# Forget bias as one f32r matmul, gates broadcast by DMA, two more ada buffers and a negated row maximum in a two-layer encoder trunk

## The chip, the cores and the metric

The kernel runs on one core of a Trainium2 chip. The metric is the device time of one execution in microseconds, lower is better. Inputs lie in HBM when it starts, and the output is written back to HBM.

## The reference

The input x is 256 x 2048 in fp32. Two layers, each a token mixer and a dense SwiGLU FFN, with six modulation vectors a layer made from the conditioning vector c:

```python
c_act = silu(c)
for i in range(2):
    mod = c_act @ ada_w[i] + ada_b[i]
    sh_a, sc_a, g_a, sh_f, sc_f, g_f = split(mod, 6)
    h = x * (1 + sc_a) + sh_a
    y = mla(h) if i == 0 else fox(h)
    x = layer_norm(ALPHA * x + (1 + g_a) * y)
    h = x * (1 + sc_f) + sh_f
    y = (silu(h @ w1) * (h @ w3)) @ w2
    x = layer_norm(ALPHA * x + (1 + g_f) * y)
```

MLA has 16 heads with a rotary part and a mask by chunks of 64. FoX (forgetting attention) has 16 heads of 128, a causal mask, and adds `cum[q] - cum[k]` to the scores, where cum is the running sum of log sigmoid of a forget logit for each head. In a softmax over k the term cum[q] falls out, so only a row of -cum[k] has to be added.

## The kernel before

Everything is computed in fp32 precision. A weight matrix comes in **units** of 256 rows by 512 columns (MLA's query weights 384), 512 KB each. SP loads a unit into one of four `raw` slots, ACT rounds it to f32r (`whi`, L503), DVE takes the rest (`wlo`, L852), and PE multiplies: activations as weights (`hT_hi`, `hT_lo`), the unit as moving data, 8 matmuls with `whi` (L1405) and 4 with `wlo` (L1411). ACT and DVE split up to four units ahead (`ahead`), each wait being on a semaphore.

The order of work on each engine is written out by hand. It goes: 16 chunks of MLA's down projection, MLA projections (32 units), MLA attention, output projection `w_o` (32 units), `norm_turn` (layer norm, turning x by PE transposes and affine), FFN (264 units), then the same with FoX. Attention runs in 19 **ticks** (`attention`), one head per tick and stage: tick i turns q and k of head i, scores head i-1, turns p of head i-2 and multiplies by v for head i-3, with units between (`gap`, by `tick_gaps`): two per tick, or six in FoX's first twelve.

Scores of a FoX head (L1579 to L1587) are four fp32 matmuls: q by k for both query tiles, and after each the bias, with 16 rows on the contraction side: a column of `ident` that picks the head, over `cumT` (16 x 256). An MLA head has the rotary part in that place (L1582). DVE adds the mask and takes the row maximum (L1189), waits for itself and multiplies by -scale (`nmax`, L1194); ACT takes exp from it (L709).

The **ada sums** are the 192 dot products of 128 rows of `ada_w` (1 MB each) with silu(c): POOL issues the loads in order (L455), each into the buffer that `ADA_SLOT` names, when the sum before in that buffer is done; DVE makes the sum (L876). The first 32 come before everything. From number 54 there are three buffers, among them `gate`, and from 64 two. The sums up to number 79 must be done before the first `norm_turn`; they stand between the other work on DVE: two a tick up to tick 16 and none in the last two, six in `w_o` and two behind it.

The **gate** (1 + g, as a column `mod`) has to stand along a row on all partitions. PE makes it by 16 fp32 matmuls of 128 columns in four parts, a broadcast column times `ident` (`gate_turn`, L1391), and ACT copies each part from PSUM (`gate_copy`, L650). This is done four times: in ticks 16 to 18 of both attentions, and in the first block of the first down product of both FFNs. DVE then uses it in `residual` (L960, L967) and `weigh` (L988). In layer 0 ACT multiplies x by ALPHA in two instructions at ticks 1 and 3 (L702); in the other sub-layers this is part of `scale_xa`.

## Time and profile before

| what | value |
|---|---|
| runs (three) | 2312.52 us median, 2311.64 to 2314.25 |
| the profiled execution: its own time, its span | 2319.15 us, 2317.4 us |
| PE busy | 2207.6 us (95%) |
| DVE, ACT busy | 1572.6 us (68%), 1009.2 us (44%) |
| HBM read | 597.49 MB, 259 GB/s over the span |
| chain of work that ended last | PE 82%, DVE 8%, DMA 7%, ACT 2%, issue 1% |

A share of busy time is a mean over stages. The stages here are: 0 to 134 us ada sums and down projection, to 303 us the MLA projections and attention up to tick 16, to 375 us its end and `w_o`, to 406 us the first norm turn, to 1128 us the first FFN, to 1510 us the FoX projections and attention, to 1556 us `w_o`, and then the second FFN to the end. Starts on PE's timeline are the better measure of a matmul's cost, since consecutive ones overlap: the row's own duration includes its way through the array.

### The profile page before, as it was taken

The page shows a single profiled execution, that of the slowest core. Times are in us where ns is not written, and L with a number is a line of the kernel's source. Part 1 is how long each engine was busy: PE and PEld are TensorE (multiplying, and loading weights), DVE is VectorE, ACT ScalarE, POOL GpSimd, SP SyncE. Part 2 cuts the span into 40 slices and gives each one's busy share as a digit, 9 for nine tenths or more (in the row PEclk, how much of TensorE's full clock was granted, in tenths as well). Part 3 has the DMA queues.
Part 4 walks back from the last instruction along what each step waited for, and adds up shares of the span by engine and source line. Part 5 has one row for each costly group of instructions (what it writes and reads, how often), then busy time and mean ns, then how long its engine had stood idle before and what let it go on. Part 6 is the DMA issues. An engine that isn't in the chain of part 4 may idle for free.

```text
span 2317.4 us, 25362 instructions
## 1 busy us (share of the span) xinstructions
PE 2207.6 (95%) x9962; PEld 1797.4 (78%) x9962; DVE 1572.6 (68%) x1799; ACT 1009.2 (44%) x1331; POOL 104.5 (5%) x207
## 2 busy tenths in 40 slices
PE   4789997999999999999999999999999999999997
PEld 2377785888888888888788888777888888888885
DVE  5779988877758777768875555568775454554556
ACT  1056644444444344444544444545444343444433
POOL 2110100000000000000000000000000000000000
PEclk9989998999999999999999999999999999999998
DMA  9988986788869888888567666656876466666563
GB/s 390 418 332 316 350 324 234 270 297 295 303 223 338 323 323 293 298 322 328 208 230 245 215 213 213 210 191 232 299 288 195 157 201 198 192 190 190 187 228 121
DMA packets 137192, 601.27 MB, mean 259 GB/s; under 512 B 15601, under 2 KB 15857, under 8 KB 111089
## 3 DMA queue, kind: packets, MB, share of 16 engines
q1 hardware_dynamic: 109424, 398.31, 49.0%
q0 software_dynamic: 27648, 201.34, 23.7%
q8 instruction: 79, 1.29, 0.2%
q14 instruction: 41, 0.33, 0.0%
HBM read 597.49 MB, written 2.10 MB: 259 GB/s over the span
## 4 chain that ended last, share of the span: by engine, by line
PE 82%; DVE 8%; DMA 7%; ACT 2%; issue 1%; POOL 0%; SPq 0%; ACTq 0%; DVEq 0%; POOLq 0%
PE ps L1405 50%; PE ps L1411 25%; DMA ada_head<-in_ada_w 4%; DVE wlo L852 2%; DVE ada_w L876 2%; PE ps L1421 2%; DMA ada_w<-in_ada_w 1%; DMA raw<-in_mla_w_o 1%; PE ps L1380 1%; PE ps L1579 1%; PE ps L1587 1%; DVE ada_wide L876 1%; PE ps L1391 1%; ACT whi L503 1%; DVE ada_head L876 1%
## 5 line engine op out<-in xcount | busy, mean ns | idle before, releaser
L852 DVE TENSOR_TENSOR wlo<-raw,whi 128x1024 fp32r<-128x1024 f32 (+2 forms) x721 | 873.4, 1217 | 641.1 <-ACT whi L503 640.4
L503 ACT ACTIVATE whi<-raw 128x1024 fp32r<-128x1024 f32 (+2 forms) x721 | 758.7, 1054 | 1096.6 <-PE ps L1411 982.5
L1405 PE MATMUL ps<-whi,hT_hi 128*128 128x512 f32 x1880 | 586.4, 393 | 0.0
L1405 PE MATMUL ps<-whi,hT_lo 128*128 128x512 f32 x1880 | 579.9, 390 | 0.0
L1411 PE MATMUL ps<-wlo,hT_hi 128*128 128x512 f32 x1880 | 502.9, 389 | 0.0
L1405 PEld LDWEIGHTS ps<-whi,hT_lo 128*128 128x128 f32 x1880 | 352.9, 188 | 74.2
L1411 PEld LDWEIGHTS ps<-wlo,hT_hi 128*128 128x128 f32 x1880 | 352.9, 188 | 74.0
L1405 PEld LDWEIGHTS ps<-whi,hT_hi 128*128 128x128 f32 x1880 | 347.9, 188 | 72.6 <-issue 3.5
L876 DVE CUSTOM_DVE_ANT_0 ada_w<-ada_w,c_bc,cols 128x2048 f32<-128x2048 f32 x153 | 358.9, 2346 | 27.8 <-DMA ada_w<-in_ada_w 27.8
L1405 PE MATMUL ps<-whi,uT_hi 128*128 128x512 f32 x672 | 208.1, 391 | 3.3 <-ACT whi L503 3.3
L1405 PE MATMUL ps<-whi,uT_lo 128*128 128x512 f32 x672 | 207.0, 389 | 0.0
L1411 PE MATMUL ps<-wlo,uT_hi 128*128 128x512 f32 x672 | 179.6, 389 | 0.0
L1405 PEld LDWEIGHTS ps<-whi,uT_hi 128*128 128x128 f32 x672 | 125.3, 188 | 29.1 <-ACT whi L503 3.6
L455 POOL DMA_DIRECT2D ada_w<-in_ada_w x153 | 80.9, 529 | 1465.2 <-DVE mod L876 1453.2
L1405 PEld LDWEIGHTS ps<-whi,uT_lo 128*128 128x128 f32 x672 | 126.1, 188 | 26.3
L1411 PEld LDWEIGHTS ps<-wlo,uT_hi 128*128 128x128 f32 x672 | 126.1, 188 | 26.3
L1701 PE MATMUL ps<-down_w,h 128*128 128x512 f32 x128 | 71.9, 689 | 22.3 <-ACT h L772 19.5
L1701 PEld LDWEIGHTS ps<-down_w,h 128*128 128x128 f32 x128 | 24.8, 216 | 43.9 <-ACT h L772 22.1
L876 DVE CUSTOM_DVE_ANT_0 ada_head<-ada_head,c_bc,cols 128x2048 f32<-128x2048 f32 x17 | 40.0, 2351 | 17.0 <-DMA ada_head<-in_ada_w 16.9
L772 ACT ACTIVATE h<-ps,mod 128x256 f32<-128x256 f32 x16 | 8.9, 564 | 84.4 <-DVE mod L876 72.3
L1421 PE MATMUL ps<-whi,hT_hi 128*128 128x512 f32 x72 | 32.5, 452 | 5.9 <-issue 3.9
L668 ACT ACTIVATE p_sb<-p_sb,pinv 128x128 f32<-128x128 f32 x64 | 25.7, 451 | 26.4 <-DVE pinv L1203 26.3
(228 smaller groups left out, 1528.0 us busy)
## 6 DMA issues: line engine op xcount, KB each, us to landing
raw<-in_ffn_w SPq DMA_DIRECT2D x528, 512.0 KB, 4.3
ada_w<-in_ada_w POOLq DMA_DIRECT2D x153, 1024.0 KB, 6.1
raw<-in_fox_w_in SPq DMA_DIRECT2D x96, 512.0 KB, 3.6
ada_head<-in_ada_w POOLq DMA_DIRECT2D x17, 1024.0 KB, 21.8
raw<-in_mla_w_o SPq DMA_DIRECT2D x32, 512.0 KB, 7.4
raw<-in_fox_w_o SPq DMA_DIRECT2D x32, 512.0 KB, 3.6
gate<-in_ada_w POOLq DMA_DIRECT2D x14, 1024.0 KB, 9.2
down_w<-in_mla_w_down SPq DMA_DIRECT2D x16, 544.0 KB, 8.0
```

The source lines that it names most:

```text
L455: pool.dma_start(ada_buffer(n), A["ada_w"][l, q, c]).then_inc(ada_in[ADA_SLOT[n]], 16)
L503: nc.scalar.activation(whi[:, s, 0:n], raw[:, s, 0:n], ACT.Copy).then_inc(hi_ready, 1)
L668: ins = nc.scalar.activation(p_sb[:, g % 2, a:b], p_sb[:, g % 2, a:b], ACT.Copy, scale=pinv[:, g % 2, t:t + 1])
L852: nc.vector.tensor_tensor(wlo[:, s, 0:n], raw[:, s, 0:n], whi[:, s, 0:n].bitcast(F32), ALU.subtract).then_inc(lo_ready, 1)
L876: nc.vector.tensor_tensor_reduce(w, w, c_bc[:, :], 1.0, adab_col[:, q, c:c + 1], ALU.mult, ALU.add, mod[:, q, c:c + 1]).then_inc(ada_done, 1)
L1380: ins = nc.tensor.transpose(ps[:, 4 + pl.turn % 2, o:o + P], tile(t, c0 + c), ident[:, :])
L1391: ins = nc.tensor.matmul(ps[:, bank, c * P:(c + 1) * P], column.to_broadcast([P, P]), ident[:, :], start=True, stop=True)
L1405: nc.tensor.matmul(ps[:, 2 * pair + t, 0:width], a[:, t * P:(t + 1) * P], w_hi, start=(first and c == 0 and a is hi), stop=False)
L1411: ins = nc.tensor.matmul(ps[:, 2 * pair + t, 0:width], hi[:, t * P:(t + 1) * P], w_lo, start=False, stop=(end and c == UC - 1))
L1421: ins = nc.tensor.matmul(ps[:, 2 * pair + t, :], a[:, t * P:(t + 1) * P], w, start=(first and c == 0 and a is hi), stop=(end and c == UC - 1))
L1579: nc.tensor.matmul(o, qkT[:, m % 2, q], qkT[:, m % 2, S:S + n], start=True, stop=False)
L1701: nc.tensor.matmul(ps[:, 2 * which + t, :], a, w[:, which * LORA:(which + 1) * LORA], start=(c == 0), stop=(c == KC - 1))
```

## The change

- **FoX bias.** `cumT` becomes `cum`, f32r, 128 rows of which 48 are used: -cum in rows 0 to 15 rounded to f32r, what the rounding left in rows 32 to 47, the three blocks of key columns (128 and 256) side by side. The cumulative sum is made for both copies from `logf_twin`. `pick` has a one in both rows of a head. One f32r matmul of 384 columns comes first in the head's scores and opens the accumulation; the two q by k matmuls add to it.
- **Gates.** `gate_turn`, `gate_copy` and `gate_parts` are gone. ACT issues a DMA (`gate_out`) that writes the column `mod` (128 x 16, fp32) as a row of 2048 into HBM, element by element, at tick 12 of both attentions and in the next to last block of each FFN's first pass, and later a DMA (`gate_in`) that reads this row onto all 128 partitions (1 MB), at tick 16 and in the first block of the down product.
- **Ada sums.** The gate buffer serves up to number 61, and 62 to 79 use four buffers: two new ones (`ada_low`, over the latents' space, free when all 32 MLA projections are done) and the two old ones. One sum stands earlier on DVE (before the latents' variance), the last two ticks have one each, `w_o` has five, and none stands behind it.
- **Maximum.** The mask pass has the factor -scale and takes the minimum, so that it gives `nmax` itself, and exp has scale -1. DVE's `nmax` instruction and its wait for itself are gone.
- **ALPHA** of layer 0 is applied in the residual's addition (`add_to`), and the two ACT instructions are gone.

```diff
@@ ada_slots
         elif n < ADA_GATE_UNTIL:
             slots.append((2, 0, 1)[(n - ADA_WIDE_UNTIL) % 3])
+        elif n < ADA_LOW_UNTIL:
+            slots.append((9, 10, 0, 1)[(n - ADA_GATE_UNTIL) % 4])
         else:
             slots.append(n % 2)
@@ constants, buffers, loads of POOL
-ADA_GATE_UNTIL = 64
+ADA_GATE_UNTIL = 62
+ADA_LOW_UNTIL = 80
+    ada_low = place_at("ada_low", [P, 2, D], F32, b0)
-    cumT = new("cumT", [H, S])
+    cum = new("cum", [P, 3 * P], F32R)
+    pick = new("pick", [P, H], F32R)
+    logf_twin = new("logf_twin", [P, T, TWIN + H])
+                if ADA_SLOT[n] >= 9:
+                    pool.wait_ge(units_used, PROJ[0])
@@ ACT
-            def gate_copy(part, bank):
...
+            def gate_out(layer, q):
+
+                act.wait_ge(ada_done, ada_end(layer, q))
+                act.dma_start(rows[pl.gate].rearrange("(c p) -> p c", p=P), mod[:, layer * MODS + q, :],
+                              allow_slow_non_contiguous=True).then_inc(gate_row, 16)
                 pl.gate += 1
+            def gate_in():
+
+                act.wait_ge(gate_row, 16 * pl.gate)
+                act.dma_start(gate[:, :], rows[pl.gate - 1].partition_broadcast(P)).then_inc(gate_copied, 16)
@@ ACT, attention
-                    if rotary and i in (1, 3):
...
-                        nc.scalar.activation(xa[:, t, :], xa[:, t, :], ACT.Copy, scale=ALPHA
-                                             ).then_inc(xa_scaled, 1)
-                                                       bias=nmax[:, m % 2, t:t + 1], scale=scale,
+                                                       bias=nmax[:, m % 2, t:t + 1], scale=-1.0,
-                    for part, bank in gate_parts(i):
...
+                    if i == H - 4:
+                        gate_out(layer, G_A)
+                    if i == H:
+                        act.wait_ge(ada_done, ada_last(2))
+                        gate_in()
@@ ACT, ffn
+                        if (n, i) == (0, nb - 2):
+                            gate_out(l, G_F)
                     if n == 0:
-                        for part in range(4):
-                            gate_copy(part, 6 + part % 2)
+                        gate_in()
@@ DVE
+            def add_to(x, y, raw):
+
+                if raw:
+                    return nc.vector.scalar_tensor_tensor(out=x, in0=x, scalar=ALPHA, in1=y,
+                                                          op0=ALU.mult, op1=ALU.add)
+                return nc.vector.tensor_tensor(x, x, y, ALU.add)
-                dve.wait_ge(gate_copied, pl.gate)
+                dve.wait_ge(gate_copied, 16 * pl.gate)
-                                p_sb[:, m % 2, a:b], ps[:, 5, a:b], mask[:, a:b], 1.0,
-                                -3.0e38, ALU.add, ALU.max, smax[:, m % 2, t:t + 1])
+                                p_sb[:, m % 2, a:b], ps[:, 5, a:b], mask[:, a:b], -scale,
+                                3.0e38, ALU.add, ALU.min, nmax[:, m % 2, t:t + 1])
-                        dve.wait_ge(masked, m + 1)
-                        nc.vector.tensor_scalar(nmax[:, m % 2, :], smax[:, m % 2, :], -scale, None,
-                                                ALU.mult).then_inc(max_ready, 1)
-                    if layer == 0 and i < TICKS - 2:
+                    if layer == 0:
                         ada()
+            ada()
             dve.wait_ge(ssq_ready, 1)
@@ PE
+                        if not rotary:
+                            nc.tensor.matmul(ps[:, 5, 0:3 * P], pick[:, i - 1:i].to_broadcast([P, P]),
+                                             cum[:, :], start=True, stop=False)
...
-                                head = ident[0:H, i - 1:i]
-                                ins = nc.tensor.matmul(o, head.to_broadcast([H, P]), cumT[:, 0:n],
-                                                       start=False, stop=True)
-                    for part, bank in gate_parts(i):
...
-                        gate_turn(layer, G_A, part, bank)
```

On PE, in the scores of one FoX head (`qkT` q and k turned, `cumT` and `cum` the bias rows). Before:

```order
L1411 MATMUL ps<-wlo,hT_hi 128x512 x4
L1579 MATMUL ps<-qkT 128x128
L1587 MATMUL ps<-cumT,ident 128x128
L1579 MATMUL ps<-qkT 128x256
L1587 MATMUL ps<-cumT,ident 128x256
L1405 MATMUL ps<-whi,hT_hi 128x512 x2
```

And now:

```order
L1423 MATMUL ps<-wlo,hT_hi 128x512 x4
L1588 MATMUL ps<-cum,pick 128x384
L1593 MATMUL ps<-qkT 128x128
L1593 MATMUL ps<-qkT 128x256
L1417 MATMUL ps<-whi,hT_hi 128x512 x2
```

The two bias matmuls are one, ahead of the q by k matmuls. On DVE, from the third residual of MLA's `w_o` to the first norm turn (the ISA rows on `mod` are the ada sums). Before:

```order
L971 BN_STATS stats<-xa 128x6 x2
L852 TENSOR_TENSOR wlo<-raw,whi 128x1024
L876 ISA ada_w,mod<-ada_w,c_bc,cols 128x2048
L876 ISA mod 128x1
L852 TENSOR_TENSOR wlo<-raw,whi 128x1024 x2
L876 ISA ada_w,mod<-ada_w,c_bc,cols 128x2048
L876 ISA mod 128x1
L852 TENSOR_TENSOR wlo<-raw,whi 128x1024
L876 ISA ada_w,mod<-ada_w,c_bc,cols 128x2048
L876 ISA mod 128x1
L876 ISA ada_w,mod<-ada_w,c_bc,cols 128x2048
L876 ISA mod 128x1
```

And now:

```order
L985 BN_STATS stats<-xa 128x6 x2
L859 TENSOR_TENSOR wlo<-raw,whi 128x1024
L883 ISA ada_low,mod<-ada_low,c_bc,cols 128x2048
L883 ISA mod 128x1
L859 TENSOR_TENSOR wlo<-raw,whi 128x1024 x3
L992 TENSOR_TENSOR gcol<-cols,mod 128x16
L994 TENSOR_TENSOR gcol<-cols,mod 128x16
L996 TENSOR_TENSOR gcol<-gcol,mod 128x16
```

Of four sums in this place one is left, and the columns of the norm turn follow the last split directly.

## Rows read from the trace of the kernel before

**Rows 1.** The page, part 1: busy time, share, instructions
```profile
PE 2207.6 (95%) x9962; PEld 1797.4 (78%) x9962; DVE 1572.6 (68%) x1799; ACT 1009.2 (44%) x1331; POOL 104.5 (5%) x207
```

**Rows 2.** Chain that ended last, in first FFN: start us, us, what
```profile
463.80 1.81 PE ps L1405 x8
466.51 1.81 PE ps L1405 x8
```

**Rows 3.** Busy us (instructions) of PE, PEld, DVE, ACT, POOL; clock; DMA share; GB/s
```profile
138.00:303.00 165.00, 152.97 (x806) 133.26 (x805) 155.70 (x258) 105.58 (x219) 17.94 (x34) 0.97 0.87 327
303.00:375.00 72.00, 65.53 (x300) 53.17 (x299) 57.99 (x66) 26.78 (x35) 5.28 (x10) 1.00 0.87 324
1167.00:1510.00 343.00, 343.00 (x1580) 275.60 (x1579) 195.41 (x277) 167.48 (x275) 11.09 (x21) 1.00 0.65 225
```

**Rows 4.** Waits of PE: total us, times, longest us
```profile
PE ps L1463 <- issue: 10.0, 3, 9.4
PE ps L1566 <- DVE hT_lo L1174: 9.7, 5, 3.8
PE ps L1421 <- DVE wlo L852: 8.2, 7, 1.7
```

**Rows 5.** PE timeline, one FoX head's scores: start us, us, instruction
```profile
1272.95 0.38 PE L1579 MATMUL ps<-qkT 128*128 128x128 f32 x2
1273.27 0.48 PE L1587 MATMUL ps<-cumT,ident 16*128 16x128 f32 x2
...
1275.50 0.63 PE L1405 MATMUL ps<-whi,hT_lo 128*128 128x512 f32 x2
```

**Rows 6.** PE timeline, one MLA head's scores
```profile
289.15 0.38 PE L1579 MATMUL ps<-qkT 128*128 128x128 f32 x2
289.37 0.39 PE L1582 MATMUL ps<-kpT,qpT 128*128 128x128 f32 x2
...
290.02 0.59 PE L1582 MATMUL ps<-kpT,qpT 128*128 128x256 f32 x2
...
290.92 0.63 PE L1405 MATMUL ps<-whi,hT_lo 128*128 128x512 f32 x2
```

**Rows 7.** PE timeline, f32r matmuls of 384 columns, two each
```profile
159.74 0.51 PE L1405 MATMUL ps<-whi,qlT_lo 128*128 128x384 f32 x2
160.09 0.51 PE L1405 MATMUL ps<-whi,qlT_hi 128*128 128x384 f32 x2
```

**Rows 8.** PE timeline, gate matmuls of first FFN
```profile
669.48 1.05 PE L1391 MATMUL ps<-ident,mod 128*128 128x128 f32 x8
...
683.10 0.73 PE L1405 MATMUL ps<-whi,uT_hi 128*128 128x512 f32 x2 [1.63 <-ACT whi L503]
```

**Rows 9.** PE timeline, gate matmuls of FoX attention
```profile
1502.92 1.95 PE L1391 MATMUL ps<-ident,mod 128*128 128x128 f32 x16
1504.62 0.70 PE L1405 MATMUL ps<-whi,hT_hi 128*128 128x512 f32 x2
```

**Rows 10.** The costliest groups of DVE, by line
```profile
L1194 DVE TENSOR_SCALAR nmax<-smax 128x2 f32<-128x2 f32 x32 | 5.4, 170 | 1.1
```

**Rows 11.** DVE timeline before the first norm turn
```profile
370.67 2.35 DVE L876 CUSTOM_DVE_ANT_0 ada_w<-ada_w,c_bc,cols 128x2048 f32<-128x2048 f32 x1 [2.22 <-DMA ada_w<-in_ada_w]
...
379.54 0.69 DVE L988 TENSOR_TENSOR sums<-ps,gate 128x512 f32<-128x512 f32 x1
```

**Rows 12.** PE timeline, start of the first and the third norm turn
```profile
384.12 1.94 PE L1463 MATMUL ps<-ident,xa 128*128 128x128 f32 x8 [9.39 <-issue]
...
1556.88 1.06 PE L1463 MATMUL ps<-ident,xa 128*128 128x128 f32 x8 [0.30 <-issue]
```

**Rows 13.** DMA: queue (packets, MB, share), issue (count, KB, us to landing)
```profile
q1 hardware_dynamic: 109424, 398.31, 49.0%
...
c_bc<-in_c SPq DMA_DIRECT2D x1, 1024.0 KB, 4.7
```

**Rows 14.** SP timeline, one small issue
```profile
1.73 0.42 SPq L368 DMA_DIRECT2D pos_i<-in_pos  x1
```

More of the change, by code:

```diff
@@ L62 @@
 FOX_CUM = 2 * PAIRS + 3
+TWIN = 32
 ADA_HEAD = 2 * KC
@@ L151, in two_pi_parts, with trunk @@
     return parts + [float(np.float32(left))]
-def trunk(nc, A, out):
+def trunk(nc, A, rows, out):
     x_d = A["x"][0].rearrange("(t p) d -> p t d", p=P)
@@ L287, in trunk @@
         down_in = [sem(f"down_in{i}") for i in range(DOWN_SLOTS)]
-        ada_in = [sem(f"ada_in{i}") for i in range(9)]
+        ada_in = [sem(f"ada_in{i}") for i in range(11)]
         raw_in = [sem(f"raw_in{i}") for i in range(RING)]
@@ L799, in _ @@
                     pl.turn += 1
-            attention(0, MLA_SCALE)
+            attention(0)
             w_o()
@@ L817, in _ @@
                     pl.turn += 1
-            attention(1, FOX_SCALE)
+            attention(1)
             w_o()
@@ L1207, in w_o @@
             def w_o(layer):
-                pl.gate += 4
-                if layer == 0:
-                    dve.wait_ge(xa_scaled, T)
+                pl.gate += 1
                 for b in range(2):
                     pl.pe += 1
-                    residual(b, True)
+                    residual(b, True, layer == 0)
                     ahead()
@@ L1218, in w_o @@
                         ada()
-                residual(2, True)
+                residual(2, True, layer == 0)
                 for k in range(PAIRS - SPLIT):
                     units(1)
-                    if layer == 0 and k in (0, 2):
+                    if layer == 0 and k == 0:
                         ada()
@@ L1353, in _ @@
                     dve.wait_ge(turned, pl.turn + 1)
-                    nc.vector.tensor_scalar(cumT[:, :], ps[0:H, 4 + pl.turn % 2, 0:S], -1 / FOX_SCALE,
-                                            None, ALU.mult).then_inc(turned_out, 1)
+                    own()
+                    for a, b in ((0, P), (P, 3 * P)):
+                        mark(nc.vector.tensor_scalar(cum[0:TWIN + H, a:b],
+                                                     ps[0:TWIN + H, 4 + pl.turn % 2, 0:b - a],
+                                                     -1 / FOX_SCALE, None, ALU.mult))
+                    own()
+                    for a, b in ((0, P), (P, 3 * P)):
+                        low = cum[TWIN:TWIN + H, a:b]
+                        ins = nc.vector.scalar_tensor_tensor(
+                            out=low, in0=ps[TWIN:TWIN + H, 4 + pl.turn % 2, 0:b - a],
+                            scalar=-1 / FOX_SCALE, in1=low.bitcast(F32), op0=ALU.mult, op1=ALU.subtract)
+                    ins.then_inc(turned_out, 1)
                     pl.turn += 1
@@ L1383, in turn @@
                 pl.turn += 1
-            def gate_turn(layer, q, part, bank):
-                pe.wait_ge(ada_done, ada_end(layer, q))
-                for c in range(4):
-                    n = 4 * part + c
-                    column = mod[:, layer * MODS + q, n:n + 1]
-                    ins = nc.tensor.matmul(ps[:, bank, c * P:(c + 1) * P],
-                                           column.to_broadcast([P, P]), ident[:, :],
-                                           start=True, stop=True)
-                ins.then_inc(gate_turned, 1)
-                pl.gate += 1
             def unit(pair, width, parts, first, end):
@@ L1825 @@
     out = nc.dram_tensor("out", (1, S, D), F32, kind="ExternalOutput").ap()
-    trunk(nc, A, out)
+    rows = nc.dram_tensor("gate_rows", (2 * LAYERS, D), F32).ap()
+    trunk(nc, A, rows, out)
     r = run_bass_kernel_spmd(nc, [{f"in_{n}": a for n, a in arrays.items()}], core_ids=[0])
```

76 lines of the change are left out of this document (29 added, 47 removed).

## The prediction

> **What bounds the kernel now.** Read the page's busy line first: PE is busy for 2207.6 us, 95% of the span [rows 1]. So nearly everywhere an instruction taken from PE shortens the run by its own pitch (start to start), and the time of DVE, ACT or the DMA queues counts only where PE idles. The chain of waits shows the steady state of an FFN: a unit every 2.71 to 2.72 us and nothing between [rows 2]. Then the windows [rows 3]. In FoX's projections and attention, to its last ticks, PE is busy for 343.00 of 343.00 us and DVE for 195.41: PE alone is the bound. In MLA's projections and attention (138 to 303 us) DVE is busy for 155.70 of 165.00 us, PE for 152.97, and DMA is 0.87 used: three resources nearly full, and none waits long for any one cause. From 303 to 375 us (last ticks and `w_o`) PE has 65.53 of 72.00 us. Last, PE's waits [rows 4]: the largest that the change touches is one of 9.4 us ahead of L1463, the first norm turn.
>
> Durations below come from the profiled execution, whose own time is 2319.15 us. The median of the runs is 2312.52, so 6.6 us less; I subtract the sum from both. About 0.2% (5 us) is what a measurement of this kernel can tell from no change.
>
> **1. FoX bias on PE.** One head's scores with the first two f32r matmuls behind them take from 1272.95 to 1275.50, so 2.55 us [rows 5]. An MLA head has four matmuls of the same columns, all with 128 rows, and takes 290.92 - 289.15 = 1.77 us for the same stretch [rows 6]. The difference, 0.78 us, is what the two bias matmuls with 16 rows cost beyond their columns. Without the second and third of the MLA matmuls there would be 0.22 us for q by k of 128 columns (289.15 to 289.37) and 0.90 us for 256 columns and the two f32r ones behind (290.02 to 290.92). The new matmul is f32r over 384 columns: two of those take 0.35 us, so 0.17 each [rows 7]. New total 0.17 + 0.22 + 0.90 = 1.29 us, 1.26 less than now. Sixteen heads: **20.2 us**. PE has no idle in this stage, so all of it counts. If the 16 rows had no price of their own, the saving would be 1.77 - 1.29 = 0.48 us a head, 7.7 us in all: the lower end. A rule stands against my reading here. The Trainium skill says in "TensorE: Matmul & The Clock Gate", section "LDWEIGHTS (loading the stationary operand)", that a 32x128 weight load takes the same time as one of 128x128. By that page the 16 rows cost nothing of their own; the 0.78 us above speaks against it.
>
> The DVE work that comes with it (a second copy of the log forget, two set-ups, three more small instructions on the cumulative sum) I cost at nothing. The cumulative sum is taken ten units after the forget logits, ten times 2.72 us, and DVE is idle for 43% of this stage [rows 3]. Without that cover it would be some 2 us, once.
>
> **2. Gates in the FFNs.** From the first gate matmul to the unit behind the last part it is 683.10 - 669.48 = 13.62 us, in which three units are done, 8.16 us [rows 2, 8]. So 5.46 us are the gate's: 16 matmuls and 1.63 us in which PE waits for ACT's split, since ACT stood at its gate copies. Two FFNs: **10.9 us**. The split then comes in time, as ACT no longer waits for PE there.
>
> **3. Gate in FoX attention.** Eight of the matmuls (16 records, as an fp32 matmul leaves two) take 1504.62 - 1502.92 = 1.70 us [rows 9]; sixteen take **3.4 us**, on PE's bound.
>
> **4. Layer 0 up to the first norm turn.** Here more than PE counts.
> - `nmax` took 0.17 us and its wait some 0.04 [rows 10]: 16 times 0.21 = 3.4 us of DVE, in a stage where DVE is 94% busy. I take 2.5. In the FoX stage it hides under PE and counts nothing.
> - The last ticks and `w_o`: 3.4 us of gate matmuls go, and some of the waits for `wlo` (8.2 us in all of the run [rows 4]), as the last four units have one ada sum beside them in place of two. Against it, two more sums (2.35 us each) stand in the last two ticks. PE has only 6.5 us of idle there [rows 3]. I take 4.0, with ends 0 and 9.
> - The norm turn: DVE still makes two sums before it, one after waiting 2.22 us for its load, and begins the norm at 379.54 [rows 11]. PE then starts 9.39 us late; in the third norm turn, with no sums before it, it is 0.30 us [rows 12]. **9.1 us** go, if the loads are there: with four buffers in place of two a load is issued two sums earlier.
> - The sum that moves ahead of the latents' variance starts some 1.5 us before DVE would have its input and takes 2.35 us: 0.9 us lost.
> - ALPHA in the addition, and the two ACT instructions less: at nothing. ACT is busy for 105.58 of 165.00 us [rows 3].
>
> Together 2.5 + 4.0 + 9.1 - 0.9 = **14.7 us**, with ends 3 (the loads are as late as now) and 21.
>
> **5. What the gate DMAs cost.** Four times, 2048 elements of 4 bytes go to HBM and 1 MB comes back. The reading part is like that of c at the start, also one row on 128 partitions, which landed after 4.7 us [rows 13]; it has 16 us or more. The writing part has no like in the trace. Per packet, queue 1 used 0.49 x 16 x 2317.4 / 109424 = 0.166 us of an engine, for 3.6 KB [rows 13]. 2048 writes are 128 on each of 16 engines, so 21 us of each if 4 bytes cost as much; if they cost only by bytes, nothing. They have four ticks or a whole block, 30 us and more, before anyone waits, and the weights' four units of 2.72 us look 10.9 us ahead. With the two in turn on an engine, the weights stay in time; I take 0, ends 0 and 3 us a gate. ACT issues it: an issue took 0.42 us for 128 small runs [rows 14]. Sixteen times as many would be 6.7 us if it goes by runs, which ACT's four units of lookahead cover but for an attention step; I take nothing here, too. The Trainium skill warns of exactly this in "DMA: Bandwidth & Descriptors", section "Rules for kernel authors": a non-contiguous last dimension "lowers to one descriptor per element". No row here shows it; what it could come to is the third rival.
>
> **Sum.** 20.2 + 10.9 + 3.4 + 14.7 = 49.2 us. Against the profiled execution's own time that gives 2270.0 us, against the median **2263.3 us**.
>
> **Rivals.**
> - *The 16 rows are free* (bias saves 7.7 us, not 20.2): 2312.5 - 36.7 = 2275.8 us. For it: only fewer columns are a sure saving. Against it: the two stretches [rows 5, 6], equal but for this. 12%.
> - *Layer 0 keeps its wait.* Number 62 may be loaded only when the 32 MLA projections are done, and the loads behind it stand in POOL's queue; with DMA 0.87 used in both windows [rows 3], more loads in flight come later, not earlier, and MLA's `w_o` units with them. Layer 0 then gives 3 us: 2312.5 - 37.5 = 2275.0 us. 18%.
> - *Slower: the element writes stand ahead of the weights.* If a 4-byte write costs a packet's time twice (a read and a write), it is 128 x 0.332 = 42.5 us on each engine. Were the weights' packets held behind them, PE would lose 42.5 - 10.9 = 31.6 us at each gate, 126 us in four, and the time would be 2312.5 - 49.2 + 126 = 2389 us. It decides from (49.2 / 4 + 10.9) / 128 = 0.18 us a write upwards, just over the 0.166 us of a packet, and only if nothing is served in between. Against it: POOL's and SP's loads are in flight together now and both land. The same page has, in its table of figures, that below 512 B the engine does read-modify-write; that would be the doubling, if it holds here. 3%.
> - *The f32r bias does not run at f32r's pace* (one broadcast column as weights, fp32 matmuls behind it in the same bank). At fp32's pace 384 columns take 0.65 us (289.37 to 290.02 is 128 and 256 columns), 0.48 more a head: 7.7 us, 2271.0 us. 5%.
>
> **How the numbers follow.** The forecast itself has 60%, its own range 2256 to 2271. The rivals on the faster side have 35%, all between 2271 and 2276; two of them together give up to 2288. The rest is the slower one and what I did not think of. The range from 2255 to 2282 leaves out the slower rival and most double misses, 2 in 10 at most. The low end is layer 0 at 21 us (2257) and a little for a clock that stays at its upper level where PE no longer idles. Faster 0.95, within 0.2% 0.02, slower 0.03.
>
> **What would show it.** The bias line: 16 matmuls (384 columns) with a pitch of 0.17 us and 1.3 us for the stretch of [rows 5]. No L1391 line, FoX's last ticks 3.4 us shorter, and in the FFNs no wait of 1.63 us behind the third unit. L1463 of the first norm turn starts within 1 us of PE's last matmul, and no sum of 2.35 us stands just ahead of the norm on DVE. PE's waits still name no DMA of the gate, and `residual` does not wait for it. Wrong: waits for `raw` in the stretches behind the four gate writes, a DVE wait for `ada_low`, or a first norm turn that starts late again.

## The result and the profile after

| | before | after |
|---|---|---|
| median (lowest to highest), four runs each | 2312.08 us (2308.39 to 2314.25) | 2276.62 us (2272.93 to 2277.93) |
| profiled execution: own time, span | 2319.15, 2317.4 us | 2275.42, 2273.5 us |

The ratio is 0.9843, with a 95% interval of 0.9831 to 0.9856. The change is faster by 35.5 us of median to median, where 49.2 were forecast. The time lies in the stated range of 2255 to 2282 us, 13.3 us above the forecast of 2263.3 and outside the forecast's own range of 2256 to 2271. From profile to profile it is 43.7 us: the profiled execution before was 7.1 us above its median, the one after 1.2 us below.

The page of the kernel after: the busy line (its like is [rows 1]), the queues, and the shares of the chain.

```profile
PE 2166.5 (95%) x9786; PEld 1771.3 (78%) x9786; DVE 1568.7 (69%) x1774; ACT 997.0 (44%) x1313; POOL 104.9 (5%) x207
...
q1 hardware_dynamic: 109424, 398.31, 50.0%
q0 software_dynamic: 27648, 201.34, 24.1%
q10 hardware_dynamic: 8832, 4.23, 0.7%
...
PE 81%; DVE 9%; DMA 8%; ACT 1%; issue 1%; POOL 0%; ACTq 0%; DVEq 0%; POOLq 0%
```

Queue 10 is the gates' own: 4 times 2048 writes and 640 other packets, 0.7% of the engines' time. Nothing in this line looks dear. The stages tell where the time went. Each norm turn's first row on PE's timeline bounds them, with the first turn of `mla_q` (the start of layer 0's attention) ahead. After:

```profile
150.30 0.38 PE L1569 MATMUL ps<-ident,mla_q 128*128 128x128 f32 x2
...
376.52 0.88 PE L1475 MATMUL ps<-ident,xa 128*128 128x128 f32 x6 [0.26 <-DVE xa L1033]
...
1115.05 0.77 PE L1475 MATMUL ps<-ident,xa 128*128 128x128 f32 x5 [0.26 <-DVE xa L1033]
1518.58 0.66 PE L1475 MATMUL ps<-ident,xa 128*128 128x128 f32 x4 [0.26 <-DVE xa L1033]
```

Before, two rows that were not yet shown (the first and the third norm turn are in [rows 12]):

```profile
154.01 0.38 PE L1558 MATMUL ps<-ident,mla_q 128*128 128x128 f32 x2
...
1128.88 0.95 PE L1463 MATMUL ps<-ident,xa 128*128 128x128 f32 x7 [0.30 <-issue]
```

| stage | before | after | less | forecast |
|---|---|---|---|---|
| to the first `mla_q` turn | 154.0 | 150.3 | 3.7 | 0 |
| layer 0 attention, `w_o`, to the norm turn | 230.1 | 226.2 | 3.9 | 14.7 |
| first FFN | 744.8 | 738.5 | 6.2 | 5.5 |
| FoX projections, attention, `w_o` | 428.0 | 403.5 | 24.5 | 23.6 |
| second FFN, to the end | 760.5 | 754.9 | 5.6 | 5.5 |

The five differences are of the two profiled executions and add up to 43.9 us. The medians differ by 8 us less, and no row says in which stage these 8 us lie.

Nothing was changed in the first stage. In the profiles of the twelve experiments it ends anywhere from 150.7 to 153.9 us, so its 3.7 us can be scatter. And its end does not carry on. In the four experiments below that change nothing in layer 0 but the gate's write, and in which it lands in time or nearly so (early write, runs of 16, half the elements, FFN gates twice), it ends at 153.55, 152.52, 152.27 and 150.75 us, and the first norm turn starts at 367.48, 367.44, 367.82 and 367.97. So the first two rows of the table belong together: 7.6 us less where 14.7 were forecast. And a stage of layer 0 by itself (213.9, 214.9, 215.6 and 217.2 us in these four) tells no difference under some 3 us, while the start of the norm turn does.

The last three stages came as forecast. In the profiles the shortfall is all in layer 0. There the norm turn no longer waits: 0.26 us in place of 9.39. But PE has a new wait, a few ticks earlier. PE's waits, after (total, times, longest; [rows 4] before), then ACT's from 250 to 340 us:

```profile
PE ps L1606 <- ACT p_sb L676: 9.3, 2, 8.2
PE ps L1577 <- DVE hT_lo L1187: 9.0, 5, 4.1
PE ps L1433 <- DVE wlo L859: 5.3, 7, 1.2
```

```profile
ACT hT_hi L684 <- DMA gate_rows<-mod: 11.1, 1, 11.1
```

The chain of work that ended last, after, from 255 to 330 us (start, us, what):

```profile
265.42 45.55 DMA gate_rows<-mod
...
311.04 0.33 ACTq L660
...
311.42 0.39 ACT hT_hi L684
...
311.84 0.42 DVE hT_lo L1187
```

At tick 16 ACT is to issue the reading of the gate's row (L660), and waits first for the writing, which it had issued at 265.4 us. That took 45.55 us, and behind ACT's wait stood its part of the attention step. PE and DVE followed: the windows have DVE at 0.61 of 11.00 us from 300 to 311 us, PE at 4.34 (in each window's line: busy us of PE, PEld, DVE, ACT and POOL, TensorE's granted clock, DMA share, GB/s).

```profile
290.00:300.00 10.00, 10.00 (x53) 8.50 (x52) 9.75 (x15) 6.36 (x16) 1.37 (x3) 1.00 1.03 331
300.00:311.00 11.00, 4.34 (x20) 3.23 (x18) 0.61 (x2) 0.28 (x1) 0.22 (x1) 0.84 0.78 316
```

The writing had 34.5 us, from 265.4 us to ACT's wait at 299.9. The three other gates' writes landed after 11.7 to 14.0 us.

PE's wait costs more than its own 8.2 us. TensorE's granted clock, 1.00 up to 307 us, is 0.50 (the level of 1.2 GHz) from 309 to 317 us, after PE had been idle from 304.3 us, and 1.00 again from 320 us. From 314.38 to 317.85 us the 512-column matmuls start 0.43 us apart, where it was 0.23 before the wait.

### The profile page after: what moved, and what is told of

It reads as the page before. It is cut to its first block, busy times and chain, and to the rows that moved or that the text cites. A ratio compares the mean times of both kernels' runs of the same rounds, so it can differ in the third digit from the quotient of the medians.

```text
span 2273.5 us, 24980 instructions
## 1 busy us (share of the span) xinstructions
PE 2166.5 (95%) x9786; PEld 1771.3 (78%) x9786; DVE 1568.7 (69%) x1774; ACT 997.0 (44%) x1313; POOL 104.9 (5%) x207
## 3 DMA queue, kind: packets, MB, share of 16 engines
q10 hardware_dynamic: 8832, 4.23, 0.7%
## 4 chain that ended last, share of the span: by engine, by line
PE 81%; DVE 9%; DMA 8%; ACT 1%; issue 1%; POOL 0%; ACTq 0%; DVEq 0%; POOLq 0%
PE ps L1417 51%; PE ps L1423 25%; DMA ada_head<-in_ada_w 5%; DVE wlo L859 2%; DMA gate_rows<-mod 2%; DVE ada_w L883 1%; PE ps L1433 1%; PE ps L1404 1%; DMA raw<-in_mla_w_o 1%; PE ps L1593 1%; DVE ada_head L883 1%; DVE ada_low L883 0%; DVE gate L883 0%; ACT whi L506 0%; DMA ada_w<-in_ada_w 0%
## 5 line engine op out<-in xcount | busy, mean ns | idle before, releaser
L883 DVE CUSTOM_DVE_ANT_0 ada_w<-ada_w,c_bc,cols 128x2048 f32<-128x2048 f32 x144 | 337.7, 2346 | 14.6 <-DMA ada_w<-in_ada_w 14.5
```

The costliest lines, as they stand in the source:

```text
L883: nc.vector.tensor_tensor_reduce(w, w, c_bc[:, :], 1.0, adab_col[:, q, c:c + 1], ALU.mult, ALU.add, mod[:, q, c:c + 1]).then_inc(ada_done, 1)
```

## The experiments

The experiments were timed in four groups, each with a median of its own for the kernel before: 2315.8 us (early write, runs of 16, 48 rows, fp32), 2315.3 (half the elements, two buffers with the late and with the early write, old places), 2313.4 (maximum, old gates, both) and 2315.4 (FFN gates twice). Ratios are against the median of the same group, so between groups they compare better than the times. Every kernel is the changed one but for the diff shown.

### The gate row written earlier, and in runs

**Early write.** Both attentions write the gate's row after tick 6:

```diff
-                    if i == H - 4:
+                    if i == 6:
```

> The changed kernel with the attention gates' write to HBM issued at tick 6 instead of tick 12; nothing else moves. Theory (the write of 2048 single elements is late): it lands some 45 us after its issue again, now well before tick 16, ACT no longer waits for it (11.1 us before), PE's wait of 8.2 us at L1606 and the one of 2.3 us behind it go, and the time falls by 8 to 11 us, to 2266 to 2269 us. Rival (ACT and PE would have waited there anyway, for ada_w loads or DVE, since DMA is 0.8 to 0.9 used): the wait moves to another releaser and the time falls by under 3 us.

Measured: 2266.95 us (2263.59 to 2275.73), ratio 0.9795 (0.9769 to 0.9820). It is 9.7 us faster than the change and the fastest kernel of the study that computes the whole reference. The first norm turn starts at 367.48 us, 9.0 us earlier than in the changed kernel and 16.6 earlier than before, where 14.7 were forecast for layer 0 (the stage from 153.55 us is 213.9 us, 16.2 less than before). PE's wait at L1606 is 0.9 us. The time came as expected, the write did not: it landed after 9.4 us in layer 0, where some 45 were expected again. At tick 6 the queue of the ada loads is not full: from 210 to 215 us 1863 writes passed beside 54 packets of it. The loads paid instead (38 GB/s from 215 to 220 us), and PE was busy for 5.00 us of these 5.

**Runs of 16.** The row is written as 128 runs of 16 elements (in another order, so the gates hold permuted values):

```diff
-rows[pl.gate].rearrange("(c p) -> p c", p=P), mod[:, layer * MODS + q, :]
+rows[pl.gate].rearrange("(p c) -> p c", p=P), mod[:, layer * MODS + q, :]
```

> The changed kernel with each gate written at its old place as 128 runs of 16 elements instead of 2048 runs of one; the 8 KB are the same, the order of the gate's elements is then another (that part of the computation is changed). Theory (each small run waits its turn behind packets of the two other queues, so the landing time goes by the number of runs): 8 runs an engine instead of 128, landing in under 8 us also in MLA's attention, no wait of ACT, time down by 8 to 11 us as in e1. Rival (a write to HBM is late there by its latency under load, whatever its runs): landing stays above 20 us, and the time within 3 us of the changed kernel.

Measured: 2266.22 us (2264.41 to 2271.3), 0.9789 (0.9770 to 0.9808). The four writes land after 3.4 to 9.0 us (9.0 in layer 0, where under 8 were expected), and ACT and L1606 wait for none. The number of elements, not the round trip through HBM, made the wait.

**Half the elements one by one.** At tick 12 as in the change:

```diff
+rows[pl.gate, 0:D // 2].rearrange("(c p) -> p c", p=P), mod[.., 0:8]
+rows[pl.gate, D // 2:D].rearrange("(p c) -> p c", p=P), mod[.., 8:16]
...
+act.wait_ge(gate_row, 32 * pl.gate)
```

> The changed kernel, its gate still written after tick 12, but only the first 1024 elements one by one; the other 1024 as 128 runs of 8 elements in a second DMA on the same queue (the gate's elements come back in another order, so the output is not the reference's). Theory (turn-taking: from 260 to 300 us both load queues are full, and an engine takes one 4-byte write, then one packet of each load queue; 45.5 us / 128 = 0.355 us a write): 64 writes per engine are 22.7 us, the element part lands near 288 us, before ACT asks for it at about 300, no wait of ACT on gate_rows, no 8 us of PE at L1606, time as with the early write, 2267 +- 3 us. Rival (the writes land when the loads' backlog ends, whatever their number): landing again near 311 us, 45 us, and 2276 us.

Measured: the part of single elements landed after 27.0 us (22.7 forecast, 45 by the rival). The runs behind it took 35.5 us, to 301.9 us, and ACT waited 1.5 us. The time is 2272.41 us (2266.75 to 2276.18), 0.9814 (0.9794 to 0.9834). So the landing came nearer the theory, and the median missed the 2267 +- 3 us that went with it. The profiled run is the fastest of the four (2266.75), and there the first norm turn starts at 367.82 us, as with the early write; what the three slower ones lost is not known. The cause of the late landing is in the queues' packets. The changed kernel, 5 us from 275 (packets, MB, share of 16 engines):

```profile
q0 software_dynamic: 192, 1.38, 66.6%
q1 hardware_dynamic: 182, 0.64, 31.5%
q10 hardware_dynamic: 192, 0.00, 2.2%
```

The half-element kernel, 5 us from 285:

```profile
q0 software_dynamic: 199, 1.46, 69.0%
q1 hardware_dynamic: 171, 0.63, 31.0%
q10 hardware_dynamic: 200, 0.00, 2.2%
```

While all queues have work, the engines take one write for one packet of the ada queue (q0) and about one of the weights' (q1). In the changed kernel that is 199, 192, 201 and 196 writes in the four stretches of 5 us from 270 to 290, beside 199, 192, 201 and 194 packets of q0 and 173, 182, 177 and 172 of q1. So a write costs its engine nearly nothing (2.2% of 80 us over 192 is 9 ns) and passes only once in 0.41 us on each engine (80 us over 197). The 64 single elements of the half-element kernel should take 26 us at this pace, and took 27.0 (the 22.7 expected were 64 times 45.5 / 128, so 0.36). All 128 would take 52 us. In the changed kernel it was 45.5 because the turns did not last to the end: 741 writes passed from 290 to 295 us, beside 136 packets of q0.

**Two ada buffers in place of four**, write at tick 12:

```diff
-ADA_GATE_UNTIL = 62
-ADA_LOW_UNTIL = 80
+ADA_GATE_UNTIL = 64
+ADA_LOW_UNTIL = 64
...
-                                act.wait_ge(ada_done, max(ada_last(9), ada_last(10)))
```

> The changed kernel (write after tick 12, all 2048 elements) without the two extra ada buffers: numbers 62 to 79 alternate between the two old ones, as before. Theory (turn-taking with full load queues): with two buffers there are at most two ada loads in flight and the queue of POOL is empty part of the time (the DMA share from 270 to 300 us is 0.83 to 0.99 in the kernel before and 1.02 in the changed one), so the writes land sooner, 25 to 38 us, and ACT waits 0 to 5 us in place of 11; against it the sums wait for their loads, and the first norm turn starts late again by some us. Time between 2270 and 2280 us. Rival (the extra loads have no part in it): landing at 45 us as now, ACT's wait of 11 us stays, and the norm's start is later than the 376.4 us of the changed kernel by the loads' lateness, 2280 us and more.

Measured: 2283.65 us (2283.39 to 2286.06), 0.9867 (0.9852 to 0.9882). The write landed after 17.3 us, shorter than the 25 to 38 forecast. It was the full queue of ada loads, which the change itself filled with its two buffers, that held the write for 45 us. But the kernel is slower, by more than expected (2270 to 2280 us): its sums wait 20.1 us for loads from 200 to 400 us, where the changed kernel's wait 3.1, and the norm turn starts at 383.74 us. And it shows a second price. Its queues in the 5 us from 275 and in the 5 us from 280:

```profile
q1 hardware_dynamic: 208, 0.73, 57.8%
q0 software_dynamic: 53, 0.30, 26.4%
q10 hardware_dynamic: 1642, 0.01, 23.6%
```

```profile
q0 software_dynamic: 43, 0.35, 92.9%
q10 hardware_dynamic: 70, 0.00, 0.8%
q1 hardware_dynamic: 3, 0.00, 0.2%
```

1642 writes pass at once, and in the next 5 us the engines are busy for 94% of the time and move 71 GB/s: 43 packets of the ada queue with 1.7 us each (92.9% of 80 us), against 0.28 us in the stretches above.

**Each FFN gate written twice.** The same slow stretch follows the FFN gates' writes in the changed kernel. Its windows (busy us of PE, PEld, DVE, ACT and POOL; clock; DMA share; GB/s):

```profile
605.00:611.00 6.00, 6.00 (x29) 4.95 (x28) 3.70 (x5) 2.34 (x3) 0.32 (x1) 1.00 0.85 296
611.00:614.00 3.00, 3.00 (x15) 2.49 (x14) 1.80 (x2) 1.34 (x2) 0.00 (x0) 1.00 1.78 184
614.00:622.00 8.00, 8.00 (x37) 6.64 (x36) 4.72 (x4) 1.62 (x2) 0.53 (x1) 1.00 0.82 65
```

ACT then waits 5.38 us for `raw`, and PE for nothing. So the FFN write was doubled, on top of the early write:

```diff
+                if q == G_F:
+                    act.dma_start(rows[pl.gate + 4].rearrange("(c p) -> p c", p=P), mod[..],
+                                  allow_slow_non_contiguous=True).then_inc(gate_twice, 16)
```

> The kernel with the early gate write, but each FFN's gate is written twice, one DMA right behind the other on the same queue (the second into rows that nobody reads). In the changed kernel the loads of the weights fall to some 30 to 90 GB/s for about 10 us behind each FFN gate's 2048 writes (612 to 622 us), ACT waits 5.4 us for raw, and PE waits for nothing, since the units look 10.9 us ahead. Theory (each 2048 writes stop the loads for about 10 us, at the edge of what the lookahead hides): 4096 writes stop them for 18 to 20 us, PE waits 7 to 11 us in each FFN, 14 to 22 us in all, time 2281 to 2289 us against 2267. Rival (the slow stretch is a fixed price of a DMA that overlaps, or the lookahead has more room than four units): PE waits under 2 us, time within 3 us of 2267.

Measured: 2280.31 us (2275.28 to 2287.55), 0.9860 (0.9831 to 0.9890), 13.4 us slower than the early write, but with a wide spread. In the profiled run, the fastest (2275.28), the loads are slow for 20 us as forecast:

```profile
605.00:625.00 20.00, 17.41 (x81) 14.01 (x79) 7.23 (x7) 4.71 (x5) 0.53 (x1) 1.00 1.01 90
```

PE waits only 2.6 us there and 3.5 in the second FFN, less than half of the 7 to 11 expected; the two FFNs are 3.2 and 5.2 us longer than with one write. The direction holds, the size doesn't, and the units that still come explain most of it. From 605 to 625 us SP's queue brought 1.59 MB, 3.0 units, which is an estimated 8.2 us of PE's work; with the 10.9 us of the four units ahead that covers 19.1 of the 20 us. The expectation had reckoned as if nothing came. One thing more was doubled than meant: the issue of the second write held ACT for 4.48 us in the first FFN and 2.50 in the second. What the slower runs lost besides stays open, as only one was profiled.

### The ada sums of layer 0

**Old places, four buffers**, with the early write: no sum ahead of the latents' variance, none in the last two ticks, two in `w_o`'s last units, and so two more behind `w_o`.

```diff
-                    if layer == 0:
+                    if layer == 0 and i < TICKS - 2:
                         ada()
...
-                    if layer == 0 and k == 0:
+                    if layer == 0 and k in (0, 2):
...
-            ada()
             dve.wait_ge(ssq_ready, 1)
```

> The kernel with the early gate write (after tick 6), but with the ada sums where they stood before: none ahead of the latents' variance, none in the last two ticks, two in w_o's last four units. The two extra buffers stay. Theory (the places matter, steps 4 of the prediction): two or three sums of 2.35 us stand between w_o and the norm again, the first norm turn starts 5 to 12 us later than the 367.5 us of the early write, and the time is 2272 to 2279 us against 2267. Rival (the buffers do it all): norm turn within 2 us of 367.5, time within 3 us of 2267.

**New places, two buffers**, with the early write; the diff is that of the buffers above.

> The kernel with the early gate write, with the sums at their new places, but without the two extra ada buffers. Theory (the loads are behind in w_o without them: DVE waited 13.1 us for six loads between 255 and 378 us in the kernel before): the sums wait for loads, 3 to 10 us in all on the norm's path, first norm turn 371 to 377 us, time 2270 to 2277 us. Rival (the places do it all): norm turn within 2 us of 367.5, time within 3 us of 2267.

**Old places and two buffers:**

> The kernel with the early gate write, without the two extra ada buffers and with the ada sums at their old places. Old places alone cost 3 us (2270.1 against 2267.0), two buffers alone 13 us (2279.8, norm turn 6 us later in the profiled run). Theory (the two are one cause, late sums: a load comes two sums too late wherever the sums stand): both together 10 to 14 us, 2277 to 2281 us. Rival (they add): 16 us and more, 2283 us and more.

| with the early write | median (lowest to highest) | ratio, interval | stage of layer 0 | first norm turn at | DVE's waits for ada loads (`ada_w` and `gate`), 200 to 400 us |
|---|---|---|---|---|---|
| new places, four buffers | 2266.95 (2263.59 to 2275.73) | 0.9795, 0.9769 to 0.9820 | 213.9 | 367.48 | 3.6 |
| old places | 2270.08 (2268.28 to 2270.85) | 0.9805, 0.9790 to 0.9820 | 216.7 | 370.31 | 3.2 |
| two buffers | 2279.83 (2272.75 to 2283.4) | 0.9849, 0.9832 to 0.9866 | 223.0 | 373.76 | 15.4 |
| both | 2280.28 (2279.95 to 2280.68) | 0.9859, 0.9844 to 0.9874 | 228.4 | 380.41 | 16.6 |

Old places alone missed my 5 to 12 us: 3.1 of the median (the intervals overlap), 2.8 of the norm turn's start. DVE waits no longer for loads there, so these 2.8 us are the sums' own time ahead of the norm. Two buffers alone cost more than expected, 12.9 us of the median, though the profiled run was its fastest and shows 6.3 us at the norm turn. There the loads are late: 15.4 us of waits in place of 3.6. Whether the two add up stays open. By the medians both together cost 13.3 us, where the single ones come to 16.0; by the ratios it is 0.0064, exactly the 0.0010 and 0.0054 of the single ones; and by the norm turn's start it is 12.9 us, more than 2.8 and 6.3. So late loads are the larger cause, and the expected one cause behind both is not shown. The norm turn in the kernel with both, and in the one with old places alone:

```profile
380.41 1.97 PE L1472 MATMUL ps<-ident,xa 128*128 128x128 f32 x8 [8.72 <-DVE xa L1031]
```

```profile
370.31 1.09 PE L1474 MATMUL ps<-ident,xa 128*128 128x128 f32 x8 [3.60 <-DVE xa L1033]
```

With both undone the wait of [rows 12] is back, 8.72 against 9.39 us. With four buffers and old places it is 3.60. With two buffers and new places it is 0.26, but PE waits for DVE in the attention instead.

### The bias

**48 rows** in place of 128, still one f32r matmul:

```diff
-pick[:, i - 1:i].to_broadcast([P, P]), cum[:, :]
+pick[0:TWIN + H, i - 1:i].to_broadcast([TWIN + H, P]), cum[0:TWIN + H, :]
```

> The changed kernel with the f32r bias matmul over only the 48 rows that are used, not 128. Theory (weights on fewer than 128 rows have a price of their own, at both neighbours, as the 16 rows had 0.78 us a head before): a head's scores get longer by 0.1 to 0.4 us, 2 to 6 us in all. Rival (only the fp32 form with few rows was dear, or the row count does not matter): within 0.05 us a head, no difference in time.

**fp32** in place of f32r, 128 rows:

```diff
-    cum = new("cum", [P, 3 * P], F32R)
-    pick = new("pick", [P, H], F32R)
+    cum = new("cum", [P, 3 * P])
+    pick = new("pick", [P, H])
```

> The changed kernel with the bias as one fp32 matmul of 384 columns over 128 rows (type fp32 for cum and pick). Theory (of the 1.26 us a head that the bias gave, 0.78 is the price of the 16 rows and 0.48 is f32r against fp32): a head gets 0.45 to 0.55 us longer than in the changed kernel, 7 to 9 us in all. Rival (the gain came from the type alone): a head gets over 1 us longer, 16 us or more.

One FoX head's scores on PE's timeline, in the changed kernel, with 48 rows, and in fp32:

```profile
1255.91 0.34 PE L1588 MATMUL ps<-cum,pick 128*128 128x384 f32 x1
1256.09 0.82 PE L1593 MATMUL ps<-qkT 128*128 128x128 f32 x4
...
1257.20 0.63 PE L1417 MATMUL ps<-whi,hT_lo 128*128 128x512 f32 x2
```

```profile
1255.84 0.43 PE L1588 MATMUL ps<-cum,pick 48*128 48x384 f32 x1
1256.20 0.92 PE L1593 MATMUL ps<-qkT 128*128 128x128 f32 x4
...
1257.42 0.40 PE L1417 MATMUL ps<-whi,hT_lo 128*128 128x512 f32 x1
```

```profile
1240.82 0.81 PE L1588 MATMUL ps<-cum,pick 128*128 128x384 f32 x2
...
1242.58 0.39 PE L1417 MATMUL ps<-whi,hT_lo 128*128 128x512 f32 x1
```

From the bias to the unit behind it that is 1.29 us in the changed kernel, 1.58 with 48 rows and 1.76 in fp32. With 48 rows the bias also starts later behind the unit ahead of it. The loads of the weights show why, in the changed kernel and with 48 rows:

```profile
1255.69 0.19 PEld L1588 LDWEIGHTS ps<-cum,pick 128*128 128x128 f32 x1
1255.91 0.59 PEld L1593 LDWEIGHTS ps<-qkT 128*128 128x128 f32 x4
```

```profile
1255.84 0.18 PEld L1588 LDWEIGHTS ps<-cum,pick 48*128 48x128 f32 x1 [0.35 <-issue]
1256.20 0.52 PEld L1593 LDWEIGHTS ps<-qkT 128*128 128x128 f32 x4 [0.18 <-issue]
```

The load of 128 rows starts 0.22 us ahead of its matmul, beside the matmul before. The load of 48 rows starts together with its matmul, after 0.35 us in which nothing was loaded, and so does the next load, after 0.18 us. Ahead of the 16 loads of 48 rows it is 5.6 us in all, with 128 rows 0.6. From the first to the seventh bias row between 1210 and 1340 us it is 110.4 us in the changed kernel and 112.8 with 48 rows, so 0.40 us a head, the top of the 0.1 to 0.4 expected. Medians: 2282.8 us (2280.39 to 2285.19), 0.9857 (0.9839 to 0.9875), and 2286.66 us (2285.31 to 2287.91), 0.9876 (0.9857 to 0.9894). Against the change's 0.9843 these are 3 and 8 us. The FoX stage is 6.2 us longer with 48 rows (16 times 0.39) and 7.4 in fp32 (16 times 0.47 by the head's rows). Here, in an experiment of its own, rows below 128 have a price beyond their columns, and f32r at 384 columns takes 0.18 us against fp32's 0.64.

### The maximum and the gates

**Maximum and negation apart again**, with the early write:

```diff
-                                3.0e38, ALU.add, ALU.min, nmax[:, m % 2, t:t + 1])
+                                -3.0e38, ALU.add, ALU.max, smax[:, m % 2, t:t + 1])
+                        dve.wait_ge(masked, m + 1)
+                        nc.vector.tensor_scalar(nmax[:, m % 2, :], smax[:, m % 2, :], -scale, None, ALU.mult)
```

> The kernel with the early gate write, but with the maximum and its negation in two instructions again (smax, then nmax). Theory (step 4: 16 times 0.21 us of DVE in a stage where DVE is full): the stretch from the first latents' turns to the first norm turn is 2.5 us longer than the early write's 213.9 us, the FoX stage is unchanged (403.5 us), time 2269.5 +- 3 us against 2267. Rival (it hides in DVE's waits and in the wait for the exponential): the stretch within 1 us of 213.9.

Measured: 2268.8 us (2266.91 to 2272.01), 0.9811 (0.9796 to 0.9826), stage of layer 0 217.4 us, FoX's 403.55. The median is 1.9 us higher and the stage 3.5 us longer, against a forecast of 2.5. But the kernel with the FFN gates twice, whose layer 0 is that of the early write, has a stage of 217.2, so the stage doesn't decide. The norm turn's start does a little better: 369.63 us, 1.7 to 2.2 us later than in the four kernels named under the stage table. That leans to the theory; from one profile it is not shown.

**Gates by PE and ACT again**, the rest as changed (`gate_turn`, `gate_copy` and `gate_parts` as in the diff of the change, with its sign turned):

```diff
-                    if i == H - 4:
-                        gate_out(layer, G_A)
-                    if i == H:
-                        act.wait_ge(ada_done, ada_last(2))
-                        gate_in()
+                    for part, bank in gate_parts(i):
...
+                        gate_copy(part, bank)
```

> The changed kernel with its four gates made by PE and copied by ACT as before; the bias, the maximum, the buffers and the places of the sums stay as changed. Theory (steps 2 to 4): against the early write's 2267 us, 10.9 us come back in the FFNs, 3.4 us in the FoX stage (406.9 in place of 403.5 us), 3 to 4 us in layer 0: 2284 to 2286 us. Rival (the elementwise writes also take bandwidth from the loads, 1863 of them in 5 us cost 19% of the engines' time and the loads' packets behind them are slow, so that part of the gain of leaving PE alone is given back): less comes back, in layer 0 nothing, 2278 to 2282 us.

Measured: 2284.43 us (2282.76 to 2287.11), 0.9881 (0.9864 to 0.9897). Stage by stage against the early write:

```profile
368.96 1.06 PE L1485 MATMUL ps<-ident,xa 128*128 128x128 f32 x8 [0.31 <-issue]
...
1113.10 0.74 PE L1485 MATMUL ps<-ident,xa 128*128 128x128 f32 x5 [0.30 <-issue]
1520.23 0.74 PE L1485 MATMUL ps<-ident,xa 128*128 128x128 f32 x5 [0.30 <-issue]
```

The first norm turn starts at 368.96 us, 1.5 later (the stage from 153.85 us is 215.1, 1.2 more), the first FFN takes 744.1 (5.6 more), FoX 407.1 (3.6 more), the second FFN 5.6 more. The total stands with the theory. In layer 0, however, only 1 to 1.5 us came back, where 3 to 4 were expected, so there the DMA way gains little even when it's early.

## Why the prediction was right or wrong

The mechanism was right for the bias, the FFN gates and FoX's gate, and wrong for the gate's write in layer 0. That the time still lies in the range is owed in part to the room that was left for rivals: by its own range, 2256 to 2271, the forecast missed. Of its signs of being wrong one came, waits for `raw` behind a gate write (5.38 us of ACT in the first FFN), and it cost PE nothing there; the wait that did cost was ACT's for `gate_rows`, which no sign named. Some 8 us between the medians and the profiles are not located.

- **Step 1, right.** FoX's stage gave 24.5 us; less the 3.6 of its gate that is 20.9 for a forecast of 20.2, and the head takes the 1.29 us that the sum had. The split into 0.78 us for the 16 rows and 0.48 for the rest was tested: 0.47 us a head for the type, 0.39 for one matmul of 48 rows. The price of 16 rows itself was not tried apart from the type. The rivals of free rows (12%) and of an f32r bias at fp32's pace (5%) fall. The page of the Trainium skill that I weighed ("TensorE: Matmul & The Clock Gate", section "LDWEIGHTS (loading the stationary operand)") speaks of the load alone, and there the trace agrees: 182 ns with 48 rows, 187 with 128. The price is in when a load starts: those of 48 rows did not run beside the matmul before.
- **Step 2, right:** 6.2 and 5.6 us less for 5.46 each, and 5.6 each came back with the old gates. The 1.63 us of [rows 8] have no like in the profile after.
- **Step 3, right:** 3.6 us for 3.4.
- **Step 4, right in the sum, and it didn't show in the change.** With the gate's row written early, the norm turn starts 16.6 us earlier than before for a forecast of 14.7. The norm turn's wait went, as the prediction had it, and mostly by the loads: four buffers are worth 13 us of the median with the places as they are (6.3 us at the norm turn in the one profile), the places alone some 3. The terms are less sure than their sum. The 4.0 us for the last ticks and `w_o` rested on 3.4 us of gate matmuls, and old gates took back only 1 to 1.5 us. Part of the gain is none of its terms: while PE waited 9.39 us, the granted clock fell to 0.50 before the norm turn of the kernel before (380 to 390 us), and with the early write it is 1.00 there. The early sum, -0.9 in the sum, wasn't tried alone. The rival that layer 0 keeps its wait (18%) named nearly the right time, 2275.0 us, and that is chance, for its reason was wrong: DVE waits for `ada_w` went from 27.8 to 14.5 us and the norm turn was on time.
- **Step 5 is the step that failed.** "They have four ticks or a whole block, 30 us and more, before anyone waits": the write took 45.5 us, and ACT waited 11.1 us with PE 8.2 us behind it. The first norm turn comes 9.0 us earlier with the early write, and the medians differ by 9.7 us. The step put its ends at 0 to 3 us a gate. It had 21 us of each engine if a write cost a packet's time, and did not add the packets that stand between the writes in turn, 2 more for each; its slower rival had nearly the time (128 x 0.332 = 42.5 us) by chance, from a packet's time taken twice, and laid it on the weights, not on the write. In layer 0 it was the reverse: the engines gave the loads their turns, and the waiting was the write's own. And the change's own extra loads filled the queues: the windows from 270 to 300 us have a DMA share of 1.02 to 1.03, against 0.83 to 0.99 before.
- **The issue on ACT** took 0.38 us for 2048 elements, so my end of 6.7 us is out for one write. A second write issued right behind held ACT longer: 0.6 to 1.5 us in the half-element kernel, 2.5 and 4.5 us with the FFN gates twice.
- **The slower rival (3%)** was nearer than its chance says. Where queues aren't full, 2048 writes pass in 2 to 3 us, and the loads are at 30 to 90 GB/s for some 8 to 10 us behind. That is some 0.08 us for each of an engine's 128 writes; the rival began to decide at 0.18. With the write doubled the slow stretch is 20 us, and PE waits a little. The Trainium skill's rule in "DMA: Bandwidth & Descriptors", section "Rules for kernel authors", of one descriptor per element is what queue 10's 8832 packets show. That read-modify-write below 512 B, which the same page of the Trainium skill states in section "Specifications", makes the slow stretch was not tested. The 128 runs of 64 B lie below 512 B too and show no slow stretch, but they are 16 times fewer.

## What to carry to other kernels

A small DMA of many elements was not priced here by its bytes or by its own engine time: it took one turn per element, and a turn was as long as the packets of the queues that were full at that moment (0.41 us with two full load queues). So ask how full the queues will be after the change, not before, and put such a write where they aren't, or well ahead of the first engine that waits; moving one line from tick 12 to tick 6 was worth 9.7 us, and the write then landed after 9.4 us in place of 45.5. An engine that other work stands behind, as ACT here, should not be the one that waits for it late. And compare two profiles by the start of a point that both must reach, not by a stage whose own start scatters.

## What the runs showed of the hardware

- **Turns per packet.** With three queues full, 4-byte writes went one for one with 7.3 KB packets (199 and 199, 192 and 192, 201 and 201 in 5 us each), one in 0.41 us on each engine, though a write occupied its engine for 9 ns.
- **A burst of scattered 4-byte writes slows the loads behind it.** After 2048 writes within about 3 us the loads fell from 296 to 65 GB/s for 8 us, with load packets of 0.74 us each (81.6% of 128 us over 141) in place of 0.15 from 605 to 611 us; in layer 0 they took 1.4 us (early write, 215 to 220 us) and 1.7 us (two buffers, 280 to 285 us). After 4096 writes it was 20 us. While the writes went in turns, from 270 to 290 us, the loads held 414 to 420 GB/s; when 741 of them passed from 290 to 295 us, the loads fell to 292.
- **48 rows cost more than 128.** A 384-column f32r matmul has 0.43 us with 48 rows and 0.34 with 128, and its stretch is 0.39 us longer, though it does the same work. The load of 48 rows starts with its matmul, after 0.35 us without a load; that of 128 rows starts 0.22 us ahead of its matmul.
- **A stall costs clock too.** After PE was idle from 304.3 us the granted clock was 0.50 from 309 to 317 us, and 512-column matmuls started 0.43 us apart in place of 0.23.
- **A second scattered write right behind the first holds the issuing engine.** The first issue took ACT 0.37 us, the second 4.48 us (2048 elements behind 2048).
